# A hybrid attention layer on eight cores: how the accumulators of two attention branches are emptied

## What is computed

```
u = rms_norm(x)
q_n, kc, vc, ks, vs, kw, vw, gate, q_f, k_f, v_f, f_l = split(u @ w_in)
o_cmp = softmax(q_n . compressed blocks of kc) @ compressed vc
o_sel = softmax(q_n . ks, the 16 best blocks of 64 by importance) @ vs
o_win = softmax(q_n . kw, the last 512 keys) @ vw
o_n   = gates[0] * o_cmp + gates[1] * o_sel + gates[2] * o_win
o_f   = forgetting_attention(q_f, k_f, v_f, f_l)
y     = g_a * (o_n @ w_branch_nsa) + g_b * (o_f @ w_branch_fox)
h     = x + y @ w_out
out   = rms_norm(h + relu(rms_norm(h) @ w_up)**2 @ w_down)
```

## Time and profile before

| | |
|---|---|
| median of 3 runs | 1173.84 us (1173.33 to 1174.19) |
| the profiled execution, its own time | 1172.47 us |
| its span, first to last instruction, slowest core | 1171.0 us |
| spans of the eight cores | 1168.5 to 1171.0 us |
| TensorE busy | 1121.3 us (96%) |
| VectorE busy | 652.6 us (56%) |
| ScalarE busy | 610.3 us (52%) |
| GpSimd busy | 73.0 us (6%) |
| mean granted TensorE clock | 0.992 to 0.997 of full speed |

### The profile page before, as it was taken

One profiled execution on the slowest core, in us unless ns is written; L12 is line 12 of the kernel. 1 busy time (PEld: TensorE's weight loads), 2 busy tenths in 40 slices (PEclk: granted clock), 3 DMA queues, 4 the chain that ended last, 5 costly groups with the idle time before them and its releaser, 6 DMA issues.

```text
span 1171.0 us, 25218 instructions; the slowest of 8 cores (1168.5 to 1171.0 us)
## 1 busy us (share of the span) xinstructions
PE 1121.3 (96%) x8607; PEld 604.9 (52%) x8607; DVE 652.6 (56%) x1482; ACT 610.3 (52%) x1248; POOL 73.0 (6%) x136
## 2 busy tenths in 40 slices
PE   2998989999999999999999999999999999999997
PEld 1555665676575757644444444444444444444443
DVE  1665767655645455633434477455656474747477
ACT  4755888999999999932222355321121202030354
POOL 1000222122110000000000000000000000000000
PEclk9998999999999999999999999999999999999999
DMA  9972000002010024172041175511121111111034
GB/s 196 216 152 51 5 10 9 6 8 44 9 30 14 3 46 78 43 254 53 1 72 37 33 121 103 105 36 37 37 37 37 36 37 36 37 37 37 1 126 162
DMA packets 36122, 70.03 MB, mean 60 GB/s; under 512 B 21312, under 2 KB 22080, under 8 KB 32032
## 3 DMA queue, kind: packets, MB, share of 16 engines
q0 software_dynamic: 5184, 34.15, 16.7%
q1 hardware_dynamic: 30816, 34.28, 10.3%
HBM read 89.38 MB, written 8.39 MB: 83 GB/s over the span
## 4 chain that ended last, share of the span: by engine, by line
PE 91%; issue 3%; DVE 2%; DMA 2%; ACT 2%; DVEq 0%; SPq 0%; POOL 0%; ACTq 0%; POOLq 0%
PE bank L328 91%; DVE RG L328 2%; DMA RG<-x 2%; ACT RG L328 2%; SPq L150 0%; POOL RG L328 0%; DVEq L167 0%; DVE arena L328 0%; DVEq L160 0%; DVE uT L328 0%; ACTq L167 0%; POOLq L167 0%
## 5 line engine op out<-in xcount | busy, mean ns | idle before, releaser
L328 ACT ACTIVATE RG<-bank 128x512 bf16<-128x512 f32 (+3 forms) x888 | 452.2, 620 | 337.3 <-PE bank L328 330.9
L328 PE MATMUL bank<-uT,arena 128*128 128x512 bf16 x2048 | 490.4, 379 | 1.3 <-DVE arena L328 0.9
L328 PE MATMUL bank<-RG 128*128 128x65 bf16 (+8 forms) x3780 | 325.2, 225 | 14.0 <-DVE RG L328 11.2
L328 PEld LDWEIGHTS bank<-uT,arena 128*128 128x128 bf16 x2048 | 199.9, 98 | 214.7 <-issue 2.5
L328 DVE TENSOR_TENSOR RG<-RG,bank 128x512 f32<-128x512 f32 x320 | 218.8, 686 | 141.1 <-PE bank L328 137.8
L328 PE MATMUL bank<-arena,RG 128*128 128x512 bf16 x1280 | 277.6, 379 | 0.0
L328 PEld LDWEIGHTS bank<-RG 128*128 128x128 bf16 (+3 forms) x3780 | 199.5, 98 | 107.1 <-issue 21.9
L328 PEld LDWEIGHTS bank<-arena,RG 128*128 128x128 bf16 x1280 | 125.3, 98 | 151.0
L328 DVE TENSOR_TENSOR RG<-RG 128x512 bf16<-128x512 f32 (+3 forms) x199 | 118.0, 594 | 151.3 <-ACT RG L328 147.3
L328 ACT ACTIVATE RG<-RG 128x512 f32<-128x512 f32 (+3 forms) x149 | 86.9, 586 | 74.2 <-DVE RG L328 46.4
L328 ACT ACTIVATE RG<-bank,prm_s 128x512 f32<-128x512 f32 x64 | 43.9, 687 | 117.5 <-PE bank L328 114.8
(11 more groups left out here) (39 smaller groups left out, 273.5 us busy)
## 6 DMA issues: line engine op xcount, KB each, us to landing
arena<-wall POOLq DMA_DIRECT2D x30, 1024.0 KB, 9.7
RG<-x SPq DMA_DIRECT2D x32, 512.0 KB, 15.9
out<-RG SPq DMA_DIRECT2D x32, 256.0 KB, 2.3
RG<-c_qx SPq DMA_DIRECT2D x8, 144.0 KB
arena<-wall POOLq DMA_DIRECT2D x4, 256.0 KB, 18.1
RG<-wall POOLq DMA_DIRECT2D x1, 1024.0 KB, 12.3
arena<-wall POOLq DMA_DIRECT2D x1, 576.0 KB, 11.0
RG<-c_kx SPq DMA_DIRECT2D x4, 144.0 KB
```

Of the source, the lines that this page charges most:

```text
L328: return P.emit(eng, lambda e, method=method, kw=kw: getattr(e, method)(**kw), ins, outs, inc)
```

## The change

In `nsa_post` the posts of the sliding and the selected branch (`br` 2 and 1, 64 of them) are written anew. One VectorE copy takes all 65 columns of the four blocks out of the bank into the scratch tile, which grows by a column. The small product and the reciprocal then read the row sums from the scratch tile, and the large product is done by GpSimd, in place, ahead of its add. The compressed branch's post and the forgetting heads' are as before.

```diff
-        RG_BYTES = 143552
+        RG_BYTES = 143680
...
-        tmpos = [cv.alloc([4, 64], F32) for _ in range(2)]
+        tmpos = [cv.alloc([4, 65], F32) for _ in range(2)]
...
-                den = Obv[ob][:, :, 64]
-                if br == 0 and tg == 0:
-                    E('dve', 'scalar_tensor_tensor', out=fs, in0=den, scalar=1e-30, in1=ginv, op0=ALU.max, op1=ALU.mult)
-                else:
-                    E('dve', 'tensor_tensor', out=fs, in0=den, in1=ginv, op=ALU.mult)
-                E('dve', 'reciprocal', out=fs, in_=fs)
                 dst = otm[:, 4 * tg:4 * tg + 4, h * 64:(h + 1) * 64]
                 if br == 0:
+                    den = Obv[ob][:, :, 64]
+                    if tg == 0:
+                        E('dve', 'scalar_tensor_tensor', out=fs, in0=den, scalar=1e-30, in1=ginv, op0=ALU.max, op1=ALU.mult)
+                    else:
+                        E('dve', 'tensor_tensor', out=fs, in0=den, in1=ginv, op=ALU.mult)
+                    E('dve', 'reciprocal', out=fs, in_=fs)
                     E('dve', 'tensor_tensor', out=dst, in0=Obv[ob][:, :, 0:64], in1=fs.unsqueeze(2).to_broadcast([128, 4, 64]), op=ALU.mult)
-                else:
-                    to = tmpos[ctr['o'] % 2]
-                    ctr['o'] += 1
-                    E('dve', 'tensor_tensor', out=to, in0=Obv[ob][:, :, 0:64], in1=fs.unsqueeze(2).to_broadcast([128, 4, 64]), op=ALU.mult)
-                    E('pool', 'tensor_tensor', out=dst, in0=dst, in1=to, op=ALU.add)
+                    return
+                to = tmpos[ctr['o'] % 2]
+                ctr['o'] += 1
+                E('dve', 'tensor_copy', out=to, in_=Obv[ob][:, :, 0:65])
+                E('dve', 'tensor_tensor', out=fs, in0=to[:, :, 64], in1=ginv, op=ALU.mult)
+                E('dve', 'reciprocal', out=fs, in_=fs)
+                E('pool', 'tensor_tensor', out=to[:, :, 0:64], in0=to[:, :, 0:64], in1=fs.unsqueeze(2).to_broadcast([128, 4, 64]), op=ALU.mult)
+                E('pool', 'tensor_tensor', out=dst, in0=dst, in1=to[:, :, 0:64], op=ALU.add)
```

## The result

| | before | after |
|---|---|---|
| median, side by side | 1173.79 us (14 runs) | 1176.89 us (14 runs) |
| ratio | | 1.0027, 95% interval 1.0019 to 1.0034 |
| the profiled execution | 1172.47 us | 1176.68 us |
| its span, slowest core | 1171.0 us | 1175.2 us |
| spans of the eight cores | 1168.5 to 1171.0 us | 1169.1 to 1175.2 us |

The change makes the kernel 3.1 us **slower** (0.27%). The forecast was 1174.0, no difference; slower had a chance of 0.30. 1176.89 lies inside the range, but outside the band of no change (1171.5 to 1176.2) that had 0.50. Some executions of every kernel are slow, with one die's cores at a lower granted clock: the medians of this text are over all executions, the ratios and their intervals leave the slow ones out, and without them the medians are at most 0.8 us lower.

The account below looks back on a forecast made before the run. TensorE, busy 96% of the span, was taken as the bound, with 9.9 us of waits for VectorE to win back. Terms -2.3 + 1.0 + 1.2 + 0.2 = +0.1 us on 1173.84 gave 1174.0 us, range 1171.0 to 1178.5.

Parts of the forecast that it names:

- band of no change: Whole kernel: a time from 1171.5 to 1176.2 us, within 0.2%, counted as no difference; chance 0.50.
- The copy ... I take 0.43: Edited posts: VectorE's 260-column copy takes 0.43 us, so each bank is free 0.60 us earlier, 64 times.
- -2.3 us: Four edited posts at 136.91, 155.95, 216.90 and 361.16 us: TensorE's bank waits shrink by 0.60, 0.60, 0.46 and 0.60 us.
- Second top-k: Second group's top-k preparation, behind a sliding post on GpSimd: the longer queue delays MAX8 and costs +1.2 us.
- First top-k: First group's top-k preparation: same instructions, but no TensorE wait for VectorE behind it; +0.2 us, bounds 0 and 0.7.
- VectorE's work stays what it was: Edited posts on VectorE: 0.99 us each against 1.03 before, 2.6 us less in all over 64.
- Cuts: Diagonal cuts near 22 posts: about 10 newly overlap GpSimd's add, 0.4 us each, 4 us more of VectorE.
- A quarter: Share of the cuts' extra 4 us of VectorE time that reaches TensorE: +1.0 us, bounds 0 and 4.
- New waits: Rings of two: small product and copy may wait for GpSimd's earlier posts; taken as nothing, upper bound 1 us.
- the blocked case: The slower rival's outcome: each overlap with GpSimd costs VectorE a full operation, +4.1 us, 1177.9 us.
- The slower rival: GpSimd blocks VectorE at 22 posts with cuts and at the small product: +5.0 + 1.4 - 2.3 us; chance 0.30.

Follow-up runs that it names:

- k3_four: f0 with the change's form only in the four posts whose bank TensorE had waited for; median 1171.54 us, ratio 0.9977.
- k1_topk_old: f1 with the two sliding posts right ahead of the top-k preparations in their old form; median 1173.37 us.
- k6_small_bank: f1 with the small product reading the row sums from the bank, behind the copy; median 1170.26 us, ratio 0.9969.
- k4_product_dve: f1 with the large product on VectorE from the scratch tile, GpSimd keeping the add alone; median 1189.79 us, ratio 1.0133.
- f1: The changed kernel with two weight loads held back until the output projection's last transposing DMA is done; median 1175.65 us.
- f0: The kernel before with two weight loads held back until the output projection's last transposing DMA is done; median 1173.88 us.
- k7_second_op: f0 with an extra GpSimd product by ones ahead of each of the 64 adds, VectorE's instructions unchanged; median 1177.73 us, ratio 1.0032.
- p49_before_pad: The kernel before with 49 one-column memsets at the head of VectorE's work, matching the changed kernel's stream length; median 1175.59 us.

## Why the prediction was right or wrong

- **"The copy ... I take 0.43"**, release 0.60 us earlier: measured 0.426, and the bank is free at the copy's end: right.
- **"-2.3 us" for four releases**: right in the places and in the sum if nothing pushes them (k3_four: 2.3); in the change 1.7, as the post at 136 us starts later than before, behind a held cut (TensorE still waits 0.71 us there). Of the other three waits 0.14 us are left at one, 0.12 at another and nothing at the third.
- **Second top-k, "+1.2"**: measured +1.2, with MAX8 waiting 2.66 us (expected about 3).
- **First top-k, "+0.2"**: the step that failed first. I argued that no wait of TensorE for VectorE stood behind it in the trace of before. The difference grows by 1.7 us from 180 to 190 us, and k1_topk_old, with the old post there, takes 0.9 of it away; at 180.00 us TensorE now waits 0.70 us for a cut that stands behind MAX8 in VectorE's queue. The absence of a wait before says nothing of the slack.
- **"VectorE's work stays what it was"**, 0.99 against 1.03 us a post: mis-sized. Behind the copy stand 0.17 us of waiting for its result, not 0.11, and the small product takes 0.17 to 0.61 us, not 0.16: 1.05 us or more. The row taken for it, 155 ns for two SBUF operands, is of operations behind the attention, where GpSimd is silent.
- **Cuts, "10 x 0.4 = 4 us"**: measured 3.2, right in size. The reading behind it was not: the three cuts of 1.03 us were taken to say that an overlap costs 0.33 us of an add of 0.72. GpSimd's add ran from 125.92 to 126.64 and the last cut ended at 126.72, 0.08 us behind it; the 0.75 us cut of 180.94 ended 0.15 us behind GpSimd's add (180.87 to 181.54). Both rows show a cut held to the end of GpSimd's operation. **"A quarter"** of VectorE's time reaching T: k6_small_bank gives 4.9 us for the 17 us that its posts are shorter, 0.28, and k4_product_dve 0.37 in the other direction. Outside the two top-k places the upward steps sum to 0.4 us (133 to 144 us), not 1.0.
- **New waits "I take nothing"**: the copy and the small product waited 2.9 us for GpSimd through the rings of two. This was not priced alone, and how much of it reached T stays open.
- The sum was +0.1, and T rose by 1.6. Only the first top-k left its bounds (0 to 0.7). That the sum was off by no more is partly luck: the first top-k was 1.5 us too low and a release 0.6 us short, the cuts 0.6 us too high. The **rest, 1.2 to 1.7 us by the medians, was in no term and in no rival**: a standstill of VectorE and a stuck DMA more than 300 us behind the last edited instruction. Without it the kernel is slower by 1.8 us (f1 against f0), which the 0.2% bound calls no difference. That the measured time stayed inside the range is the width of the range, which reached to 1178.5 for another reason, the blocked case. The slower rival named GpSimd's blocking as its mechanism; k7_second_op gives that 2.2 us, where the rival had 6.4 (5.0 + 1.4) before the release was taken off. So the side that came true was there, with a third of its price.
- The two rules of the Trainium skill. The Trainium skill, "VectorE: DVE Perf Modes", section on the TRN2 errata, has VectorE's fixed cost lower from SBUF: no row of the 64 posts shows it. The small product takes 188 ns in the mean from SBUF (166 in the median) beside 157 from the bank, and the large product took 426 ns from SBUF (k4_product_dve) and 424 from the bank. The Trainium skill, "SBUF — State Buffer", section "SBUF: two separate sides", has the pair of ports as an exclusive lock held for the whole instruction, and the traces agree: the small product of 0.61 us and all held cuts end just behind GpSimd's operation, and what starts ahead of it isn't held. The rival took a full GpSimd operation of 0.7 us for each of 22 posts. The lock costs only what is left of the operation: the cuts' mean rises by 53 ns over 64 of them in k7_second_op, since only some start inside one.

## What to carry to other kernels

Count a post by how long it keeps its engine, gaps included, and not by when it frees the bank: on VectorE, put an operation that doesn't need the last result directly behind it (the row sums can be read from the bank after the copy as well), before trading time to another engine. An operation with two SBUF operands that starts while GpSimd works on SBUF is held until GpSimd's operation ends, so look at which of the two comes first (0.28 us or up to 0.80 for the same cut); with one operand in the bank it was never held (64 small products of 152 ns, at most 154, in k6_small_bank). A gain of the release belongs only to the places where TensorE waits for that bank; four posts of 64 gave 2.3 us, which is all that the prediction had found. And before a loss of 0.1% is put down to an edit, pad the instruction stream of the kernel before by as many records as the change adds.

## What the hardware showed that I had not expected

- VectorE stands still without a cause that its queue shows at fixed places of its instruction stream. In the 14 kernels' traces I found 205 such standstills of 0.16 to 0.39 us behind 100 us of the span, and every one is at a record whose number (counted from the core's first VectorE record) is 59, 60 or 61 above a multiple of 128. Not every such place has one; that it takes a busy VectorE to show it is a guess. That it is the fetching of the next instructions is another: the count of packets in the page's instruction queues doesn't follow it (p49_before_pad has the standstill and before's 48 packets in queue 14, the change has 49).
- A transposing DMA on SP's queue that was issued 1.63 us or more behind the second of two 1-MB loads of GpSimd's queue stayed in issue for 8 to 11 us instead of 1.3 (24 cores); one at 1.41 to 1.44 us passed, and the next was stuck (16 cores).
- TensorE's granted clock can fall in the middle of the attention, and not on every core: at the 2.5 us wait near 210 us of k4_product_dve on eight cores, at the one near 169 us on two, at about 1.5 us of T each.
- VectorE's instructions overlap by 0.08 us where the later one doesn't need the earlier, and stand 0.1 to 0.17 us apart where it does; over 64 posts this was worth more than the whole change.
